# A four-layer network on one core: the split operands are placed at a different byte distance from the weights in each stage

## The chip, the core and the metric

The kernel runs as one program on one of the eight cores of a Trainium2 chip. Its time is device microseconds (us) from launch to end; lower is better. The engines named below are TensorE (PE; PEld is its weight load), VectorE (DVE), ScalarE (ACT), GpSimd (POOL) and SyncE (SP), which issues the DMAs.

## What is computed

A sequence of 256 tokens with 1024 channels goes through four residual layers, each a mixer and then a feed-forward block, all in float32:

```
for mixer, ffn in ((moba, conv_ffn), (mla, conv_ffn), (pool, conv_ffn_2), (chunk_attention, conv_ffn_2)):
    h = h + mixer(rms_norm(h))
    h = h + ffn(rms_norm(h))

def conv_ffn(xn, w_gate, conv_w, conv_b, w_up, w_down):        # 1024 -> 2816 -> 1024
    g = xn @ w_gate
    gc = conv_b + sum(conv_w[j] * shifted(g, j) for j in range(3))
    return (gelu(gc) * (xn @ w_up)) @ w_down
```

The three attention mixers have 16 heads of 64; the second works through low-rank latents (384 and 256 wide); the pool mixer takes means over 2, 4, 8 and 16 tokens and then one 256x256 product per group of channels. A final norm lies between the second and the third layer.

## The kernel before

**Stages.** The program has eight stages, numbered `A, F0, B, F1, POOL, F2, DD, F3`: A, B and DD are the attention mixers, POOL the pool mixer, F0 to F3 the feed-forward blocks. They run one after the other, since each needs the residual stream of the one before. Each engine has a hand-written program (`tensor_program`, `scalar_program`, `vector_program`, `sync_program`), and semaphores tie them together; no scheduler orders anything.

**Weights.** All weights come as 180 units of up to 128x2048 floats (1 MB). SP loads them into three buffers `raw`. ScalarE copies a unit to `whi` in the format fp32r (line 1173), VectorE writes the rest, `raw - whi`, to `wlo` (line 1712). `whi` and `wlo` are rings of five buffers of 8192 bytes per partition each.

**Split operands.** The other operand is split in the same way, each 256 columns of high part followed by 256 columns of low part: `xx` holds the stage's normalised input (8 blocks of 128 channels, lines 1176 and 1717), `hx` the activations of a feed-forward block (22 blocks, lines 1248 and 1863), `ox` the outputs of the attention heads, and in stage B the latents (8 blocks, lines 1311 and 1956). A product is high times high, plus high times low, plus low times high.

**The three ways in which TensorE takes them.** In `block_wide` (lines 463 and 465) the weights are stationary: one matmul streams the 512 columns of high and low part against 128x128 of `whi`, and one the 256 columns of the high part against `wlo`. Such a pair is the unit of almost all work in F0 to F3 and of half the output projection of the attention mixers. In `across` and `last_pair` (helper `three`, lines 422 to 424) it is three matmuls of 256 columns. In the query, key and value products of A and DD (lines 679, 680 and 686) the roles are the other way round: 128x128 of `xx` is stationary and 512 columns of `whi` or `wlo` stream. Lines 518 and 519 sum squares for the norm: `sx`, 256 columns, streams against the constant `ones_r`.

**Where the buffers lie.** Buffers follow each other in a partition in the order of the code, each at a multiple of 32 bytes. Every `whi` and `wlo` begins at a multiple of 128 bytes. `gx`, ahead of `xx`, is 8 floats longer than a multiple, so `xx` begins 32 bytes past a multiple of 128. An unused buffer of 8 floats (`pad_moving`) stands ahead of `vec`, and with it `sx`, `ones_r`, `hx` and `ox` begin 32 bytes past a multiple of 128 too. All slices that a matmul takes begin a multiple of 512 bytes further on in their buffer. "Distance" below is the start of the split operand less that of the weights, modulo 128 bytes: 32 in every stage of this kernel. `sx` and `ones_r` have the distance 0 to each other.

Of the kernel before, what the change touches and what calls it, by code (L numbers as in the profile page):

```python
# [7 lines left out]
F32 = mybir.dt.float32  # L8
F32R = mybir.dt.float32r
# [6 lines left out]
NF = 22  # L16
# [24 lines left out]
A, F0, B, F1, POOL, F2, DD, F3 = range(8)  # L41

# [58 lines left out]
def build(nc, dram, out):  # L101
    plan, first = unit_plan()
    N_UNITS = len(plan)
    with ExitStack() as ctx:
# [55 lines left out]
        xx = sb("xx", [128, KD, 2, S], F32R)  # L160
# [15 lines left out]
        hx = sb("hx", [128, NF, 2, S], F32R, ffn_mem)  # L176
# [10 lines left out]
        ox = sb("ox", [128, KD, 2, S], F32R, att_mem)  # L187
# [30 lines left out]
        TB = ctx.enter_context(nc.psum_tensor("TB", [128, 2, 512], F32))  # L218

# [43 lines left out]

        def xh(k):
            return xx[:, k, 0, :]

        def xl(k):
            return xx[:, k, 1, :]
# [151 lines left out]
        def tensor_program(e):  # L420
# [51 lines left out]
            def last_pair(s):  # L472


                b = ffn_banks(s, 5)
                for m in range(2):
                    kk = 0
                    for n, nk in zip(range(first[s] + 31, first[s] + 34), (8, 8, 6)):
                        wh, wl = unit(n)
                        if m == 0:  # L480
                            weights_here(n)
                        for k in range(nk):
                            start, stop = kk == 0, kk == NF - 1
                            if m == 0:
                                last = block_wide(n, b[:, 0, :], 0, k, hx, kk, start, stop)
                            else:
                                last = three(b[:, 1, 0:256], wh[:, k, 128:256], wl[:, k, 128:256], hx[:, kk, 0, :],
                                             hx[:, kk, 1, :], start, stop)
# [39 lines left out]
            def ffn(s):  # L528
                u = first[s]
                bg, bu = ffn_banks(s, 0), ffn_banks(s, 1)  # L530
                weights_here(u + 1)
                if s != F2:
                    e.wait_ge(s_res, n_res(s - 1, 1))
                if s == F2:
                    for k in (0, 1):
                        x_here(s, k)
                        across_wide(u, bg, k, xx, k, k == 0, False)
                    e.wait_ge(s_uu, 2)
                    for k in (0, 1):
                        across_wide(u + 1, bu, k, xx, k, k == 0, False)  # L540
                for k in range(2 if s == F2 else 0, KD):
                    x_here(s, k)
                    last = across_wide(u, bg, k, xx, k, k == 0, k == KD - 1)
                    if k == KD - 1:
                        last.then_inc(s_used, 1)
                    last = across_wide(u + 1, bu, k, xx, k, k == 0, k == KD - 1)
                    if k == KD - 1:
                        last.then_inc(s_used, 1)
                if s != F2:
                    spread_sums(s)  # L550
                for i in range(1, 11):
                    n = u + 2 * i
                    bg, bu = ffn_banks(s, 2 * i), ffn_banks(s, 2 * i + 1)
                    weights_here(n)
                    if i >= 2:
                        e.wait_ge(s_gr, n_ff(s, i - 2))
                    for k in range(KD):
                        last = across_wide(n, bg, k, xx, k, k == 0, k == KD - 1)
                        if s == F2 and i == 1 and k == 0:
                            spread_sums(s)  # L560
                    last.then_inc(s_used, 1)
                    weights_here(n + 1)
                    if i >= 2:
                        e.wait_ge(s_ub, n_ff(s, i - 2))
                    else:
                        e.wait_ge(s_sr, LAYER[s] + 1)
                    for k in range(KD):
                        last = across_wide(n + 1, bu, k, xx, k, k == 0, k == KD - 1)
                    last.then_inc(s_used, 1)
                n = u + 22  # L570
                for c in range(4):
                    b = ffn_banks(s, 2 + c)
                    e.wait_ge((s_gr, s_ub)[c % 2], n_ff(s, 9 + c // 2))
                    if c == 3:
                        last_pair(s)
                        break
                    k0 = 0
                    for j, nk in enumerate((8, 8, 6)):
                        weights_here(n)
                        for k in range(nk):  # L580
                            if c == 0:
                                e.wait_ge(s_hl, n_ff(s, (k0 + k) // 2))
                            last = across_wide(n, b, k, hx, k0 + k, k0 + k == 0, k0 + k == NF - 1)
                        last.then_inc(s_used, 1)
                        n += 1
                        k0 += nk
# [65 lines left out]
            def project(s, u, c, ks):  # L652
# [4 lines left out]
                for k in ks:  # L657
                    last = across_wide(u + c, out_banks(c), k, ox, k, k == 0, k == KD - 1)
# [3 lines left out]
            def heads_mixer(s):  # L662
# [10 lines left out]
                def high(i, h, k):  # L673
# [5 lines left out]
                    e.matmul(po, xx[:, k, 0, sl], wh[:, k % 4, :], start=k == 0, stop=False, skip_group_check=True)  # L679
                    e.matmul(po, xx[:, k, 1, sl], wh[:, k % 4, :], start=False, stop=False, skip_group_check=True)  # L680

                def low(i, h, k):
# [3 lines left out]
                    return e.matmul(slot_bank(s, i, h)[:, :], xx[:, k, 0, sl], wl[:, k % 4, :], start=False,  # L686
# [194 lines left out]
            def latent_mixer():  # L881
# [3 lines left out]
                def latent_half(i, h):  # L885
# [10 lines left out]
                    for k in range(4):  # L896
# [3 lines left out]
                        last = three(b[:, 0:w], xx[:, kk, 0, sl], xx[:, kk, 1, sl], wh[:, k, :], wl[:, k, :],  # L900
# [28 lines left out]
                def channels(n, b, col, nk, kk, at):  # L929
# [3 lines left out]
                    for m in range(2):  # L933
                        sl = slice(col + m * 128, col + (m + 1) * 128)
                        for k in range(nk):
                            last = three(po[:, m, :], wh[:, k, sl], wl[:, k, sl], ox[:, kk + k, 0, :],
                                         ox[:, kk + k, 1, :], m == 0 and k == 0, k == nk - 1)
# [12 lines left out]
                def value_block(h, c):  # L950
# [10 lines left out]
                    for k in range(2):  # L961
                        last = three(bk(s, 2 + (h if c == 0 else 0))[:, :], ox[:, 6 + k, 0, sl], ox[:, 6 + k, 1, sl], wh[:, k, :],
# [3 lines left out]
                def query_rope(h):  # L966
# [7 lines left out]
                    for k in range(3):  # L974
                        last = three(bk(s, h)[:, :], ox[:, 3 + k, 0, sl], ox[:, 3 + k, 1, sl], wh[:, k, :], wl[:, k, :],
# [44 lines left out]
                def rows(c, *ks):  # L1020

                    for k in ks:
# [4 lines left out]
                        last = across(u + 10 + c, out_bank(s, c), k, ox, k, k == 0, k == KD - 1)  # L1027
# [64 lines left out]
            def pool_mixer():  # L1092
# [22 lines left out]
                def linear(g):  # L1115
# [3 lines left out]
                    for k in (2 * g, 2 * g + 1):  # L1119
                        x_here(s, k)  # L1120
                        for h in range(2):
                            sl = slice(h * 128, (h + 1) * 128)
                            last = three(b[:, h * 256:(h + 1) * 256], xx[:, k, 0, sl], xx[:, k, 1, sl], wh[:, k, :],
# [34 lines left out]
        def scalar_program(e):  # L1158
# [16 lines left out]
            def split_x(s, k):  # L1175
                e.activation(xx[:, k, 0, :], xT[:, k, :], ACT.Copy, scale=gain_of(s, k)).then_inc(s_xh, 1)
# [63 lines left out]
            def ffn(s, func):  # L1240
# [5 lines left out]
                def finish(i):  # L1246
                    e.wait_ge(s_hb, n_ff(s, i))
                    e.activation(hx[:, 2 * i:2 * i + 2, 0, :], hb[:, :, :], ACT.Copy).then_inc(s_hh, 1)
# [60 lines left out]
            def output_hi(s, j):  # L1309
                e.wait_ge(s_av, n_pair(s, j))  # L1310
                e.activation(ox[:, j, 0, :], av_bank(s, j)[:, 0:256], ACT.Copy).then_inc(s_oh, 1)
# [162 lines left out]
            def latent_mixer():  # L1474
# [38 lines left out]
                def latent_hi(t, c):  # L1513
                    gain = vcol("b_q_norm", c) if c < 3 else vcol("b_kv_norm", c - 3)
                    e.wait_ge(s_lt, t + 1)
                    e.activation(ox[:, 3 + c, 0, :], LT[t % 3], ACT.Copy, scale=gain).then_inc(s_ch, 1)
# [179 lines left out]
        def vector_program(e):  # L1696
# [18 lines left out]
            def split_x(s, k):  # L1715
                e.wait_ge(s_xh, n_x(s, k))
                e.scalar_tensor_tensor(out=xx[:, k, 1, :], in0=xT[:, k, :], scalar=gain_of(s, k),  # L1717
                                       in1=xx[:, k, 0, :].bitcast(F32), op0=ALU.mult,
# [124 lines left out]
            def ffn(s):  # L1843
# [17 lines left out]
                def low(i):  # L1861
                    e.wait_ge(s_hh, n_ff(s, i))
                    e.tensor_tensor(hx[:, 2 * i:2 * i + 2, 1, :], hb[:, :, :],
                                    hx[:, 2 * i:2 * i + 2, 0, :].bitcast(F32), ALU.subtract).then_inc(s_hl, 1)
# [270 lines left out]
            def latent_mixer():  # L2135
# [14 lines left out]
                def latent_lo(t, c):  # L2150
                    gain = vcol("b_q_norm", c) if c < 3 else vcol("b_kv_norm", c - 3)
                    e.wait_ge(s_ch, t + 1 if t < 2 else t)
                    e.scalar_tensor_tensor(out=ox[:, 3 + c, 1, :], in0=LT[t % 3], scalar=gain,
                                           in1=ox[:, 3 + c, 0, :].bitcast(F32), op0=ALU.mult,
# [318 lines left out]
```

## Time and profile before

| | |
|---|---|
| median of 3 runs | 1072.65 us (1072.24 to 1073.18) |
| profiled execution, first to last instruction | 1070.4 us, 2.25 us under the median of the runs |
| PE busy | 1064.7 us (99%), 6536 matmuls |
| PE weight loads busy | 932.3 us (87%) |
| DVE busy | 839.0 us (78%) |
| ACT busy | 655.2 us (61%) |
| DMA | 191.67 MB, mean 179 GB/s |
| share of PE in the chain that ended last | 94% |

The profiled execution has no run time of its own on record beside its span, so the span is set against the median of the three runs; what lies between is launch and end. Matmuls are pipelined: the duration that the profile shows for one (0.39 us) overlaps the next, so the pace is read from the distance of two starts, not from durations.

### The profile page before, as it was taken

Reading aid. Unit: us, or ns where it says so; the run is one execution under the profiler, and the core shown is the slowest. Engines: PE = TensorE matmul, PEld = TensorE weight load, DVE = VectorE, ACT = ScalarE, POOL = GpSimd, SP = SyncE. Lnnn points to the kernel's source line nnn. Section 1 sums busy time; section 2 is a strip of 40 time slices with the busy share of each in tenths; the row PEclk is TensorE's granted clock in tenths of the full one; section 3 lists DMA queues with packets and bytes.
Section 4 is the critical chain, followed back from the end, with each engine's and each line's share of the span. In section 5 each row is a group of like instructions: output and inputs, shape, how many; then the busy total and the mean of one; then the engine's idle time right before and its main releaser. Section 6 shows DMA issues by size and latency. Waiting matters only on the chain.

```text
span 1070.4 us, 16292 instructions
## 1 busy us (share of the span) xinstructions
PE 1064.7 (99%) x6536; PEld 932.3 (87%) x6536; DVE 839.0 (78%) x1364; ACT 655.2 (61%) x922; POOL 1.3 (0%) x8
## 2 busy tenths in 40 slices
PE   9999999999999999999999999999999999999998
PEld 7778888888898888888889888888877788888888
DVE  7985799886668779987667999876668768997852
ACT  7666567665458766765556577654456765776540
POOL 0000000000000000000000000000000000000000
PEclk9999999999999999999999999999999999999999
DMA  9552446555426155655552466455555533665540
GB/s 339 181 180 114 156 164 233 195 186 216 163 83 252 55 180 190 230 202 181 214 195 81 151 215 229 182 217 187 187 177 182 174 106 140 236 220 190 206 142 30
DMA packets 32091, 191.67 MB, mean 179 GB/s; under 512 B 4496, under 2 KB 6160, under 8 KB 12176
## 3 DMA queue, kind: packets, MB, share of 16 engines
q1 hardware_dynamic: 32016, 190.62, 50.3%
q8 instruction: 52, 0.85, 0.3%
q14 instruction: 23, 0.19, 0.1%
HBM read 189.56 MB, written 1.05 MB: 178 GB/s over the span
## 4 chain that ended last, share of the span: by engine, by line
PE 94%; DVE 2%; ACT 2%; issue 1%; DMA 0%; SPq 0%; DVEq 0%; ACTq 0%
PE banks L463 21%; PE TB L463 12%; PE SB L463 11%; PE banks L465 11%; PE TB L465 6%; PE SB L465 6%; PE banks L679 4%; PE banks L686 4%; PE banks L680 4%; PE banks L422 3%; PE banks L424 3%; PE banks L423 3%; PE banks L636 2%; PE TB L610 2%; PE SB L597 1%
## 5 line engine op out<-in xcount | busy, mean ns | idle before, releaser
L1712 DVE TENSOR_TENSOR wlo<-raw,whi 128x2048 fp32r<-128x2048 f32 (+2 forms) x180 | 395.8, 2201 | 78.6 <-ACT whi L1173 78.5
L1173 ACT ACTIVATE whi<-raw 128x2048 fp32r<-128x2048 f32 (+2 forms) x180 | 330.5, 1840 | 81.3 <-PE TB L465 25.6
L463 PE MATMUL banks<-xx,whi 128*128 128x512 f32 x752 | 262.2, 390 | 0.2 <-DVE wlo L1712 0.2
L465 PE MATMUL banks<-xx,wlo 128*128 128x256 f32 x752 | 212.1, 282 | 0.0
L463 PEld LDWEIGHTS banks<-xx,whi 128*128 128x128 f32 x752 | 141.2, 188 | 30.0 <-DVE wlo L1712 0.5
L465 PEld LDWEIGHTS banks<-xx,wlo 128*128 128x128 f32 x752 | 142.1, 189 | 0.0
L463 PE MATMUL TB<-xx,whi 128*128 128x512 f32 x336 | 117.8, 390 | 0.2 <-DVE xx L1717 0.2
L463 PE MATMUL SB<-xx,whi 128*128 128x512 f32 x320 | 111.8, 390 | 0.0
L465 PE MATMUL TB<-xx,wlo 128*128 128x256 f32 x336 | 94.7, 282 | 0.0
L463 PE MATMUL banks<-hx,whi 128*128 128x512 f32 x264 | 91.7, 390 | 0.0
L465 PE MATMUL SB<-xx,wlo 128*128 128x256 f32 x320 | 90.2, 282 | 0.0
L1258 ACT ACTIVATE ct<-gp,vec 128x256 f32<-128x256 f32 x88 | 48.2, 595 | 63.1 <-DVE gp L1879 63.1
L679 PE MATMUL banks<-whi,xx 128*128 128x512 f32 x192 | 78.0, 406 | 0.5 <-ACT whi L1665 0.5
L680 PE MATMUL banks<-whi,xx 128*128 128x512 f32 x192 | 75.9, 395 | 0.0
L463 PEld LDWEIGHTS TB<-xx,whi 128*128 128x128 f32 x336 | 63.1, 188 | 13.5 <-issue 0.3
L465 PE MATMUL banks<-hx,wlo 128*128 128x256 f32 x264 | 74.4, 282 | 0.0
L463 PEld LDWEIGHTS SB<-xx,whi 128*128 128x128 f32 x320 | 60.1, 188 | 12.6
L465 PEld LDWEIGHTS TB<-xx,wlo 128*128 128x128 f32 x336 | 63.5, 189 | 0.0
L463 PE MATMUL TB<-hx,whi 128*128 128x512 f32 x176 | 61.2, 390 | 0.0
L463 PE MATMUL SB<-hx,whi 128*128 128x512 f32 x176 | 61.2, 390 | 0.0
L465 PEld LDWEIGHTS SB<-xx,wlo 128*128 128x128 f32 x320 | 60.5, 189 | 0.0
L463 PEld LDWEIGHTS banks<-hx,whi 128*128 128x128 f32 x264 | 49.6, 188 | 10.4
(244 smaller groups left out, 1944.6 us busy)
## 6 DMA issues: line engine op xcount, KB each, us to landing
raw<-in_gate SPq DMA_DIRECT2D x44, 1024.0 KB, 4.7
raw<-in_up SPq DMA_DIRECT2D x44, 1024.0 KB, 4.8
raw<-in_down SPq DMA_DIRECT2D x32, 1024.0 KB, 4.8
raw<-in_down SPq DMA_DIRECT2D x16, 768.0 KB, 4.2
raw<-in_d_kq SPq DMA_DIRECT2D x8, 1024.0 KB, 5.0
raw<-in_a_kq SPq DMA_DIRECT2D x6, 1024.0 KB, 5.8
raw<-in_a_o SPq DMA_DIRECT2D x4, 1024.0 KB, 4.8
raw<-in_b_o SPq DMA_DIRECT2D x4, 1024.0 KB, 5.6
```

Source lines behind the costliest of these rows:

```text
L422: e.matmul(po, ah, bh, start=start, stop=False, skip_group_check=True)
L423: e.matmul(po, ah, bl, start=False, stop=False, skip_group_check=True)
L424: return e.matmul(po, al, bh, start=False, stop=stop, skip_group_check=True)
L463: e.matmul(po[:, 0:512], wh[:, k, sl], a[:, kk, :, :].rearrange("p w s -> p (w s)"), start=start, stop=stop, skip_group_check=True)
L465: return e.matmul(po[:, 0:256], wl[:, k, sl], a[:, kk, 0, :], start=False, stop=stop, skip_group_check=True)
L610: last = e.transpose(TB[:, a, c * 128:(c + 1) * 128], sc[:, a, c * 128:(c + 1) * 128], ident)
L679: e.matmul(po, xx[:, k, 0, sl], wh[:, k % 4, :], start=k == 0, stop=False, skip_group_check=True)
L680: e.matmul(po, xx[:, k, 1, sl], wh[:, k % 4, :], start=False, stop=False, skip_group_check=True)
L686: return e.matmul(slot_bank(s, i, h)[:, :], xx[:, k, 0, sl], wl[:, k % 4, :], start=False, stop=k == KD - 1, skip_group_check=True)
L1173: e.activation(whi[n % RING][:, 0:nk * w], raw[n % RAW][:, 0:nk * w], ACT.Copy).then_inc(s_hi, 1)
L1258: e.activation(ct[:, m, :], g[:, m, 0:S], ACT.Identity, scale=cw(0, 2 * i + m), bias=cb(2 * i + m)).then_inc(s_tap, 1)
L1712: e.tensor_tensor(wlo[n % RING][:, 0:nk * w], raw[n % RAW][:, 0:nk * w], whi[n % RING][:, 0:nk * w].bitcast(F32), ALU.subtract).then_inc(s ...
```

## The change

`xx`, `hx` and `ox` become flat buffers that are 32 floats (128 bytes) longer. Each stage takes a view into them (`XX[s]`, `HX[s]`, `OX[s]`) that begins at an offset of its own, in floats, from three tables. Every read and write of the three buffers on TensorE, ScalarE and VectorE goes through the view of its stage. The number, order, shapes and waits of all instructions stay as they are. Buffers allocated behind `xx` move by 128 bytes, those behind `hx` or `ox` by 256, so their place modulo 128 bytes stays.

```diff
+SHIFT = 32
+X_AT = {A: 16, F0: 4, B: 4, F1: 8, POOL: 0, F2: 12, DD: 8, F3: 16}
+H_AT = {F0: 20, F1: 24, F2: 28, F3: 0}
+O_AT = {A: 2, B: 1, DD: 6}
...
-        xx = sb("xx", [128, KD, 2, S], F32R)
+        xx = sb("xx", [128, KD * 2 * S + SHIFT], F32R)
...
-        hx = sb("hx", [128, NF, 2, S], F32R, ffn_mem)
+        hx = sb("hx", [128, NF * 2 * S + SHIFT], F32R, ffn_mem)
...
-        ox = sb("ox", [128, KD, 2, S], F32R, att_mem)
+        ox = sb("ox", [128, KD * 2 * S + SHIFT], F32R, att_mem)
...
+        def placed(buf, n, at):
+            return buf[:, at:at + n * 2 * S].rearrange("p (k w s) -> p k w s", k=n, w=2)
+
+        XX = {st: placed(xx, KD, X_AT[st]) for st in range(8)}
+        HX = {st: placed(hx, NF, H_AT[st]) for st in (F0, F1, F2, F3)}
+        OX = {st: placed(ox, KD, O_AT[st]) for st in (A, B, DD)}
...
-                                last = block_wide(n, b[:, 0, :], 0, k, hx, kk, start, stop)
+                                last = block_wide(n, b[:, 0, :], 0, k, HX[s], kk, start, stop)
...
-                    last = across_wide(u, bg, k, xx, k, k == 0, k == KD - 1)
+                    last = across_wide(u, bg, k, XX[s], k, k == 0, k == KD - 1)
...
-                        last = across(u + c, bk(s, c), k, ox, k, k == 0, k == KD - 1)
+                        last = across(u + c, bk(s, c), k, OX[s], k, k == 0, k == KD - 1)
...
-                    e.matmul(po, xx[:, k, 0, sl], wh[:, k % 4, :], start=k == 0, stop=False, skip_group_check=True)
+                    e.matmul(po, XX[s][:, k, 0, sl], wh[:, k % 4, :], start=k == 0, stop=False, skip_group_check=True)
...
-                e.activation(xx[:, k, 0, :], xT[:, k, :], ACT.Copy, scale=gain_of(s, k)).then_inc(s_xh, 1)
+                e.activation(XX[s][:, k, 0, :], xT[:, k, :], ACT.Copy, scale=gain_of(s, k)).then_inc(s_xh, 1)
...
-                e.tensor_tensor(ox[:, j, 1, :], av_bank(s, j)[:, 0:256], ox[:, j, 0, :].bitcast(F32),
+                e.tensor_tensor(OX[s][:, j, 1, :], av_bank(s, j)[:, 0:256], OX[s][:, j, 0, :].bitcast(F32),
```

The rest of the diff puts the views in place of the buffers in the same way, and removes two unused helpers. With the 32 bytes that the buffers had already, the distances from the weights are, in bytes:

| stage | A | F0 | B | F1 | POOL | F2 | DD | F3 |
|---|---|---|---|---|---|---|---|---|
| `xx` | 96 | 48 | 48 | 64 | 32 | 80 | 64 | 96 |
| `hx` | | 112 | | 0 | | 16 | | 32 |
| `ox` | 40 | | 36 | | | | 56 | |

## Rows read from the trace of the kernel before

**Rows 1.** Page, parts 1 and 2: busy share of engines, TensorE clock
```profile
PE 1064.7 (99%) x6536; PEld 932.3 (87%) x6536; DVE 839.0 (78%) x1364; ACT 655.2 (61%) x922; POOL 1.3 (0%) x8
...
PEclk9999999999999999999999999999999999999999
```

**Rows 2.** Waits of TensorE (PE) over the whole span
```profile
PE SB L670 <- DVE ones L2297: 1.1, 1, 1.1
PE banks L679 <- ACT whi L1665: 0.5, 1, 0.5
PE banks L636 <- ACT pt L1307: 0.4, 1, 0.4
PE banks L463 <- DVE wlo L1712: 0.2, 1, 0.2
PE TB L463 <- DVE xx L1717: 0.2, 1, 0.2
```

**Rows 3.** Timeline, stage F0, PE: start us, duration us, instruction
```profile
200.13 0.39 PE L463 MATMUL TB<-xx,whi 128*128 128x512 f32 x1
200.36 0.28 PE L465 MATMUL TB<-xx,wlo 128*128 128x256 f32 x1
200.48 0.39 PE L463 MATMUL TB<-xx,whi 128*128 128x512 f32 x1
...
202.56 0.39 PE L463 MATMUL TB<-xx,whi 128*128 128x512 f32 x1
```

**Rows 4.** Timeline, end of F3, PE (line 422 begins each group of three)
```profile
1061.33 0.28 PE L422 MATMUL banks<-hx,whi 128*128 128x256 f32 x1
...
1062.38 0.28 PE L422 MATMUL banks<-hx,whi 128*128 128x256 f32 x1
```

**Rows 5.** Timeline, stage DD, PE
```profile
784.59 0.40 PE L679 MATMUL banks<-whi,xx 128*128 128x512 f32 x1
...
785.06 0.40 PE L679 MATMUL banks<-whi,xx 128*128 128x512 f32 x1
```

**Rows 6.** Groups by shape, PE: count | busy us, mean ns | idle before
```profile
L463 PE MATMUL banks<-xx,whi 128*128 128x512 f32 x752 | 262.2, 390 | 0.2 <-DVE wlo L1712 0.2
L465 PE MATMUL banks<-xx,wlo 128*128 128x256 f32 x752 | 212.1, 282 | 0.0
...
L680 PE MATMUL banks<-whi,xx 128*128 128x512 f32 x192 | 75.9, 395 | 0.0
...
L422 PE MATMUL banks<-ox,whi 128*128 128x256 f32 x136 | 39.7, 292 | 0.0
...
L422 PE MATMUL banks<-hx,whi 128*128 128x256 f32 x88 | 24.5, 279 | 0.0
...
L463 PE MATMUL SB<-ox,whi 128*128 128x512 f32 x48 | 16.9, 391 | 0.0
...
L518 PE MATMUL SB<-sx,ones_r 128*128 128x256 f32 x4 | 1.1, 281 | 0.0
```

**Rows 7.** Timeline around lines 518 and 519, stage F1, PE
```profile
400.65 0.28 PE L465 MATMUL banks<-xx,wlo 128*128 128x256 f32 x1
400.77 0.28 PE L518 MATMUL SB<-sx,ones_r 128*128 128x256 f32 x1
400.89 0.28 PE L519 MATMUL SB<-sx,ones_r 128*128 128x256 f32 x1
```

**Rows 8.** Busy time in a stretch, line 463 alone, stage F1
```profile
389.60:573.00 183.40, 175.59 (x507) 94.96 (x506) 1.00 0.54 194
```

**Rows 9.** Groups by shape, PE, stage DD alone
```profile
L680 PE MATMUL banks<-whi,xx 128*128 128x512 f32 x96 | 38.0, 395 | 0.0
```

**Rows 10.** Groups by shape, VectorE (DVE)
```profile
L1887 DVE SCALAR_TENSOR_TENSOR ct<-gp,vec,ct 128x256 f32<-128x256 f32 x88 | 38.4, 477 | 0.0
L1891 DVE SCALAR_TENSOR_TENSOR ct<-gp,vec,ct 128x256 f32<-128x256 f32 x88 | 38.4, 477 | 0.0
...
L1717 DVE SCALAR_TENSOR_TENSOR xx<-gx,vec,xx 128x256 fp32r<-128x256 f32 x48 | 21.3, 481 | 7.8 <-ACT xx L1176 7.8
```

More of the change, by code:

```diff
@@ L262, in unit @@
                     wlo[r][:, 0:nk * w].rearrange("p (k n) -> p k n", k=nk))
[L264 to L268, printed above, removed]
         def gain_of(s, k):
@@ L484, in last_pair @@
                             if m == 0:
-                                last = block_wide(n, b[:, 0, :], 0, k, hx, kk, start, stop)
+                                last = block_wide(n, b[:, 0, :], 0, k, HX[s], kk, start, stop)
                             else:
-                                last = three(b[:, 1, 0:256], wh[:, k, 128:256], wl[:, k, 128:256], hx[:, kk, 0, :],
-                                             hx[:, kk, 1, :], start, stop)
+                                last = three(b[:, 1, 0:256], wh[:, k, 128:256], wl[:, k, 128:256], HX[s][:, kk, 0, :],
+                                             HX[s][:, kk, 1, :], start, stop)
                             kk += 1
@@ L557, in ffn @@
                     for k in range(KD):
-                        last = across_wide(n, bg, k, xx, k, k == 0, k == KD - 1)
+                        last = across_wide(n, bg, k, XX[s], k, k == 0, k == KD - 1)
                         if s == F2 and i == 1 and k == 0:
@@ L567, in ffn @@
                     for k in range(KD):
-                        last = across_wide(n + 1, bu, k, xx, k, k == 0, k == KD - 1)
+                        last = across_wide(n + 1, bu, k, XX[s], k, k == 0, k == KD - 1)
                     last.then_inc(s_used, 1)
@@ L582, in ffn @@
                                 e.wait_ge(s_hl, n_ff(s, (k0 + k) // 2))
-                            last = across_wide(n, b, k, hx, k0 + k, k0 + k == 0, k0 + k == NF - 1)
+                            last = across_wide(n, b, k, HX[s], k0 + k, k0 + k == 0, k0 + k == NF - 1)
                         last.then_inc(s_used, 1)
@@ L657, in project @@
                 for k in ks:
-                    last = across_wide(u + c, out_banks(c), k, ox, k, k == 0, k == KD - 1)
+                    last = across_wide(u + c, out_banks(c), k, OX[s], k, k == 0, k == KD - 1)
                 if ks[-1] == KD - 1:
@@ L678, in high @@
                     po = slot_bank(s, i, h)[:, :]
-                    e.matmul(po, xx[:, k, 0, sl], wh[:, k % 4, :], start=k == 0, stop=False, skip_group_check=True)
-                    e.matmul(po, xx[:, k, 1, sl], wh[:, k % 4, :], start=False, stop=False, skip_group_check=True)
+                    e.matmul(po, XX[s][:, k, 0, sl], wh[:, k % 4, :], start=k == 0, stop=False, skip_group_check=True)
+                    e.matmul(po, XX[s][:, k, 1, sl], wh[:, k % 4, :], start=False, stop=False, skip_group_check=True)
                 def low(i, h, k):
@@ L685, in low @@
                     sl = slice(h * 128, (h + 1) * 128)
-                    return e.matmul(slot_bank(s, i, h)[:, :], xx[:, k, 0, sl], wl[:, k % 4, :], start=False,
+                    return e.matmul(slot_bank(s, i, h)[:, :], XX[s][:, k, 0, sl], wl[:, k % 4, :], start=False,
                                     stop=k == KD - 1, skip_group_check=True)
@@ L899, in latent_half @@
                             x_here(s, kk)
-                        last = three(b[:, 0:w], xx[:, kk, 0, sl], xx[:, kk, 1, sl], wh[:, k, :], wl[:, k, :],
+                        last = three(b[:, 0:w], XX[s][:, kk, 0, sl], XX[s][:, kk, 1, sl], wh[:, k, :], wl[:, k, :],
                                      kk == 0, kk == KD - 1)
@@ L935, in channels @@
                         for k in range(nk):
-                            last = three(po[:, m, :], wh[:, k, sl], wl[:, k, sl], ox[:, kk + k, 0, :],
-                                         ox[:, kk + k, 1, :], m == 0 and k == 0, k == nk - 1)
+                            last = three(po[:, m, :], wh[:, k, sl], wl[:, k, sl], OX[s][:, kk + k, 0, :],
+                                         OX[s][:, kk + k, 1, :], m == 0 and k == 0, k == nk - 1)
                     return last
@@ L961, in value_block @@
                     for k in range(2):
-                        last = three(bk(s, 2 + (h if c == 0 else 0))[:, :], ox[:, 6 + k, 0, sl], ox[:, 6 + k, 1, sl], wh[:, k, :],
+                        last = three(bk(s, 2 + (h if c == 0 else 0))[:, :], OX[s][:, 6 + k, 0, sl], OX[s][:, 6 + k, 1, sl], wh[:, k, :],
                                      wl[:, k, :], k == 0, k == 1)
@@ L974, in query_rope @@
                     for k in range(3):
-                        last = three(bk(s, h)[:, :], ox[:, 3 + k, 0, sl], ox[:, 3 + k, 1, sl], wh[:, k, :], wl[:, k, :],
+                        last = three(bk(s, h)[:, :], OX[s][:, 3 + k, 0, sl], OX[s][:, 3 + k, 1, sl], wh[:, k, :], wl[:, k, :],
                                      k == 0, k == 2)
@@ L1026, in rows @@
                         e.wait_ge(s_ol, n_pair(s, k))
-                        last = across(u + 10 + c, out_bank(s, c), k, ox, k, k == 0, k == KD - 1)
+                        last = across(u + 10 + c, out_bank(s, c), k, OX[s], k, k == 0, k == KD - 1)
                         if k == KD - 1:
@@ L1122, in linear @@
                             sl = slice(h * 128, (h + 1) * 128)
-                            last = three(b[:, h * 256:(h + 1) * 256], xx[:, k, 0, sl], xx[:, k, 1, sl], wh[:, k, :],
+                            last = three(b[:, h * 256:(h + 1) * 256], XX[s][:, k, 0, sl], XX[s][:, k, 1, sl], wh[:, k, :],
                                          wl[:, k, :], k == 2 * g and h == 0, k == 2 * g + 1)
@@ L1716, in split_x @@
                 e.wait_ge(s_xh, n_x(s, k))
-                e.scalar_tensor_tensor(out=xx[:, k, 1, :], in0=xT[:, k, :], scalar=gain_of(s, k),
-                                       in1=xx[:, k, 0, :].bitcast(F32), op0=ALU.mult,
+                e.scalar_tensor_tensor(out=XX[s][:, k, 1, :], in0=xT[:, k, :], scalar=gain_of(s, k),
+                                       in1=XX[s][:, k, 0, :].bitcast(F32), op0=ALU.mult,
                                        op1=ALU.subtract).then_inc(s_xl, 1)
@@ L2152, in latent_lo @@
                     e.wait_ge(s_ch, t + 1 if t < 2 else t)
-                    e.scalar_tensor_tensor(out=ox[:, 3 + c, 1, :], in0=LT[t % 3], scalar=gain,
-                                           in1=ox[:, 3 + c, 0, :].bitcast(F32), op0=ALU.mult,
+                    e.scalar_tensor_tensor(out=OX[s][:, 3 + c, 1, :], in0=LT[t % 3], scalar=gain,
+                                           in1=OX[s][:, 3 + c, 0, :].bitcast(F32), op0=ALU.mult,
                                            op1=ALU.subtract).then_inc(s_cl, 1)
```

16 lines of the change are left out of this document (8 added, 8 removed).

## The prediction

> **What bounds the kernel now.** I read the page first: TensorE is busy for 99% of the span, and its granted clock is full, 1.0, which is the 2.4 GHz level, in all 40 slices [rows 1]. Then the waits of TensorE. They name all that it ever waited for, and the five of them sum to 1.1 + 0.5 + 0.4 + 0.2 + 0.2 = 2.4 us [rows 2]. So no producer, buffer or DMA decides anything here; the time is the pace at which TensorE takes its matmuls, and a change can show only if it changes that pace or makes a new wait longer than the slack that now hides it.
>
> The pace is in the timeline. In F0 seven pairs (512 columns against `whi`, then 256 against `wlo`) begin between 200.13 and 202.56, which is 0.347 us a pair; the first takes 0.23 and the second 0.12 [rows 3]. At one column per cycle of 2.4 GHz, 768 columns would take 0.320 us, so a pair loses 0.027 us, 8%. The groups of three at the end of F3 take 0.35 us for 768 columns (three groups in 1.05 us) [rows 4], and the mixer products with the roles reversed 0.47 us for two matmuls of 512 columns, 0.235 us each [rows 5]. All pay 8 to 10% over the column count. What this change can touch is this surplus: it alters neither the number nor the order of instructions, only where the streamed operand starts against the stationary one.
>
> **The change, part by part.** *TensorE.* The question is whether the distance between the two operands sets the surplus. The trace before has three cases. Distance 32 with the weights stationary: 390 ns for 512 columns, 282 ns for 256 in a pair, 279 ns for 256 in a group of three. The same buffers with the roles reversed, so that the weights stream: 395 ns for 512 columns. And distance 0, `sx` against `ones_r`: 281 ns for 256 columns [rows 6]. In the timeline that matmul starts 0.12 us after its predecessor and its successor 0.12 us after it, as for every other matmul of 256 columns [rows 7]. So going from distance 32 to 0 shows nothing above 2 or 3 ns on 256 columns, and there are only four such matmuls, each in the midst of others. I take 0 ns per matmul for every new distance, since the only other distance in the trace is the one nearest to a test of the change.
>
> The bounds. Above: the largest step that the rows show between two placements or roles is 5 ns on 512 columns (395 less 390) and 3 ns on 256 (282 less 279) [rows 6]. All pairs but those on `hx` in F3 and all the reversed products get a new distance. The four feed-forward blocks have some 506 pairs each (the stretch of F1 holds 507 of line 463, one at its edge) [rows 8], the mixers 2 x 48 on `ox` [rows 6], so 2120 in all, and 154 of them (`hx` in F3, 7 passes of 22) stay: 1966 pairs x 8 ns = 15.7 us. The reversed products are 3 x 96 in DD [rows 9] and as many in A: 576 x 5 ns = 2.9 us. Together +18.6 us, if every distance but 32 paid the full step. Below: the whole surplus of 27 ns a pair [rows 3] taken back in every pair would be -53 us; in a single block of 506 pairs, -13.7 us. I take 0 between these ends, since the row at distance 0 lies on the present pace, and not between it and either end.
>
> The Trainium skill speaks on both sides. "SBUF — State Buffer" (section "SBUF: two separate sides") gives TensorE a second independent read port for the weight load, by which the distance would not matter at all and the sum stays 0. The same page (Specifications) says that each cross to a new 16-byte line pays a penalty. All offsets of `xx` and `hx` keep the number of such lines, but `ox` at 36, 40 and 56 bytes takes one line more per stream; an estimate from that page, one line in 64 of some 80 us of `ox` streams, is 1.3 us. No run here shows it yet.
>
> *ScalarE and VectorE.* They write the buffers and VectorE reads the high part back. VectorE reads `gp` 4 bytes on in line 1887 and 8 bytes on in line 1891: both take 477 ns, and the same shape written into `xx` 481 ns [rows 10]. So 0 ns for an odd start. If an access to `ox` were slower all the same, VectorE is busy 78% and ScalarE 61% of the span [rows 1], and TensorE's wait for them sums to 2.4 us [rows 2]; that slack is the cover. Without it, 24 pieces of `ox` in three mixers would have to be some 90 ns slower each to reach 2.2 us.
>
> *DMA and memory.* No DMA touches the three buffers. The buffers behind them move by 128 or 256 bytes, so nothing changes modulo 128.
>
> The sum is 0. The profiled execution spans 1070.4 us, 2.25 us under the median of the runs, and I forecast the median: 1072.7 us.
>
> **The rivals.** *Slower, by the distance 0.* The weight load of the next matmul runs while the present one streams, and two readers at the same place in a line or bank could hold each other up. Three uses land on a multiple of 64 bytes: `xx` and `hx` in F1 and `xx` in DD. For it speaks that the surplus exists at all and is the same in every feed-forward block, which all have one distance; against it the matmul at distance 0 [rows 6, 7]. Price with the steps above: 506 pairs x 8 ns = 4.0 us, and 288 x 5 ns = 1.4 us, so 1078.1 us. The place to see it is F1 against F0. It decides from about 4 ns a pair on, where it reaches 2.1 us, 0.2%; that is about what a measurement of this kernel can tell from no change. Chance 0.20.
>
> *Slower, as every distance but 32 pays.* Then every block but the `hx` part of F3 slows, up to 1072.7 + 18.6 = 1091.3 us; at half the step, 1082. Chance 0.12.
>
> *Slower, by the offsets of `ox` alone*, which are the only ones that are no multiple of four floats. No matmul in the trace streams from such a start. If those streams went at half pace, 96 pairs x 0.347 and 3 x 136 matmuls x 0.117 us [rows 3, 4, 6] would come a second time, +81 us; a tenth of it would be 1080.8 us. VectorE's indifference to such starts [rows 10] speaks against it. Chance 0.08.
>
> *Faster.* The distance 32 may be a poor one. If one of the new distances freed a block of its surplus, this block would go from 0.347 to 0.320 us a pair, -13.7 us, 1059 us; a tenth of the surplus in all pairs would be -5.3 us, 1067.4 us. The trace speaks against it only by the matmul at distance 0, which is no faster. The skill's "TensorE: Matmul & The Clock Gate" (section "Back-to-back issue gap") gives N/2.4 + 2.5 ns for a matmul, 325 ns for a pair by an estimate from it; the trace's 347 disagrees, so something does hold fp32r back. Chance 0.14.
>
> *No change*, within 0.2%: 0.46, the forecast.
>
> **How the numbers follow.** Faster has the 0.14 of its case, no change 0.46, and slower 0.20 + 0.12 + 0.08 = 0.40. For the range I leave out about half of the faster case (below 1067) and the worse half of the second and third case (above 1085), some 0.17 in all: 1067 to 1085 us. The forecast's own range is 1070.6 to 1074.8.
>
> **What would show it.** Right: a pair takes 0.347 us in F0, F1, F2 and F3 alike, the mixers keep 0.235 us and 0.117 us, and each stage has the length that it has now. The first rival shows as F1 longer than F0 with DD longer than A, at an unchanged mean for lines 422 to 424 on `ox`; the second as an even stretch of all blocks with the `hx` part of F3 at the old pace; the third as longer means of the rows on `ox` alone; the last as a block whose pair comes nearer to 0.320 us. The forecast is wrong if any block's pair moves by more than 4 ns, or if a wait of TensorE for `ox` or `xx` above 2 us appears that is not there now.

## The result and the profile after

The changed kernel takes 1083.01 us (median of 3 runs, 1082.39 to 1083.21) against 1072.65 us: ratio 1.0096, 95% interval 1.0082 to 1.011. It is slower by 10.4 us, 1%. The profiled execution spans 1080.6 us, 10.2 us more than before.

Parts 1 and 2 of the page after, engines and clock, answer to [rows 1]:

```profile
PE 1075.6 (100%) x6536; PEld 932.8 (86%) x6536; DVE 839.7 (78%) x1364; ACT 655.1 (61%) x922; POOL 1.3 (0%) x8
...
PEclk9999999999999999999999999999999999999999
```

The waits of TensorE after, all that there are, answer to [rows 2]:

```profile
PE SB L676 <- DVE ones L2303: 1.1, 1, 1.1
PE banks L642 <- ACT pt L1313: 0.3, 1, 0.3
PE TB L469 <- DVE xx L1723: 0.2, 1, 0.2
```

TensorE is still busy all the time, at the same clock and with the same 6536 matmuls, but for 10.9 us longer (1075.6 less 1064.7); its waits are 1.6 us in place of 2.4. The busy time of VectorE and ScalarE is the same within 0.7 us. So nothing waits for anything new: the matmuls themselves are taken more slowly. The lines have moved by 6: 463, 465, 422, 518 and 680 are now 469, 471, 428, 524 and 686. The groups by shape after (count | busy us, mean ns), which answer to [rows 6]:

```profile
L469 PE MATMUL banks<-xx,whi 128*128 128x512 f32 x752 | 265.4, 395 | 0.1
L471 PE MATMUL banks<-xx,wlo 128*128 128x256 f32 x752 | 210.8, 280 | 0.0
...
L469 PE MATMUL banks<-hx,whi 128*128 128x512 f32 x264 | 92.6, 394 | 0.0
...
L686 PE MATMUL banks<-whi,xx 128*128 128x512 f32 x192 | 76.3, 397 | 0.0
...
L428 PE MATMUL banks<-ox,whi 128*128 128x256 f32 x136 | 40.0, 294 | 0.0
...
L524 PE MATMUL SB<-sx,ones_r 128*128 128x256 f32 x4 | 1.1, 280 | 0.0
```

The 512 columns of a pair have gone from 390 to 395 ns on `xx` (394 on `hx`), the 256 columns from 282 to 280; the reversed product from 395 to 397. Durations overlap, so the pace is better read from starts. In the timeline of F1 after (start us, duration us), on `hx`, the first and the twelfth 512-column matmul of a run:

```profile
529.82 0.40 PE L469 MATMUL TB<-hx,whi 128*128 128x512 f32 x1
...
533.71 0.40 PE L469 MATMUL TB<-hx,whi 128*128 128x512 f32 x1
```

Eleven pairs in 3.89 us are 0.3536 us a pair, where [rows 3] give 0.347. The same reading over every pair of a stage, and over all other matmuls on the three buffers, says where the 10.2 us went. Change of the summed times from start to start, in us:

| | A | F0 | B | F1 | POOL | F2 | DD | F3 | sum |
|---|---|---|---|---|---|---|---|---|---|
| on `xx` | +0.46 | +1.20 | +0.04 | +2.31 | -0.16 | +1.05 | +0.07 | +1.17 | +6.1 |
| on `hx` | | +1.05 | | +1.24 | | 0.00 | | +0.05 | +2.3 |
| on `ox` | +0.53 | | +1.05 | | | | +0.26 | | +1.8 |

The sum, 10.3 us, is the whole difference. Every stage with a new distance pays, except F2 on `hx` (distance 16); the products with the roles reversed, on `xx` in A, B and DD, pay little. The groups of three pay most for their length: between the starts of two groups on `ox` there were 350.0 to 351.0 ns and are now 360.2 (A, DD) and 361.2 ns (B), and on `hx` in F1 there are 360.0 for 350.0.

### The profile page after: what moved, and what is told of

Same layout as the page of the kernel before. It is cut to its first block, busy times and chain, and to the rows that moved or that the text cites. A ratio compares the mean times of both kernels' runs of the same rounds, so it can differ in the third digit from the quotient of the medians.

```text
span 1080.6 us, 16292 instructions
## 1 busy us (share of the span) xinstructions
PE 1075.6 (100%) x6536; PEld 932.8 (86%) x6536; DVE 839.7 (78%) x1364; ACT 655.1 (61%) x922; POOL 1.3 (0%) x8
## 3 DMA queue, kind: packets, MB, share of 16 engines
HBM read 189.56 MB, written 1.05 MB: 176 GB/s over the span
## 4 chain that ended last, share of the span: by engine, by line
PE 97%; DVE 1%; ACT 1%; issue 0%; DVEq 0%
PE banks L469 21%; PE TB L469 12%; PE SB L469 12%; PE banks L471 11%; PE TB L471 6%; PE SB L471 6%; PE banks L685 4%; PE banks L686 4%; PE banks L692 4%; PE banks L428 3%; PE banks L429 3%; PE banks L430 3%; PE banks L642 2%; PE TB L616 2%; PE SB L603 1%; PE banks L761 1%
## 5 line engine op out<-in xcount | busy, mean ns | idle before, releaser
L469 PE MATMUL banks<-xx,whi 128*128 128x512 f32 x752 | 265.4, 395 | 0.1
L469 PE MATMUL TB<-xx,whi 128*128 128x512 f32 x336 | 119.1, 395 | 0.2 <-DVE xx L1723 0.2
```

The costliest lines, as they stand in the source:

```text
L469: e.matmul(po[:, 0:512], wh[:, k, sl], a[:, kk, :, :].rearrange("p w s -> p (w s)"), start=start, stop=stop, skip_group_check=True)
```

## The experiments

The theory: TensorE's pace depends on where the streamed operand begins relative to the weights. The rivals: it depends on the absolute place of the streamed operand; the longer buffers and higher addresses do it; one reader alone (the load of the next weights, or the matmul's own weights) sets the loss. "A pair" below is the mean time from one 512-column start to the next, over all pairs of the stage named that follow each other directly, from the starts in that run's trace; three or four pairs of F2 that hold a wait or the sums of the norm are left out. All medians stand beside runs of the kernel before on the same chip, 1072.4 to 1072.5 us.

**Longer buffers alone.**

```diff
-X_AT = {A: 16, F0: 4, B: 4, F1: 8, POOL: 0, F2: 12, DD: 8, F3: 16}
-H_AT = {F0: 20, F1: 24, F2: 28, F3: 0}
-O_AT = {A: 2, B: 1, DD: 6}
+X_AT = {A: 0, F0: 0, B: 0, F1: 0, POOL: 0, F2: 0, DD: 0, F3: 0}
+H_AT = {F0: 0, F1: 0, F2: 0, F3: 0}
+O_AT = {A: 0, B: 0, DD: 0}
```

> The changed kernel with all three tables at 0: the buffers are longer and what lies behind them has moved by 128 and 256 bytes, but every distance is 32 as before. If the distance modulo 128 bytes sets the pace, or the absolute place modulo 128 does: 1072.7 us, a pair (512 and 256 columns) at 0.347 us. If the lengthening itself, by higher address bits, made the loss: near 1083 us.

Measured: 1072.91 us, ratio 1.0004 (0.9995 to 1.0014). The lengthening costs nothing; the offsets do it. `xx` keeps 228.4 + 118.3 ns a pair to the tenth. `hx`, which the longer `xx` has moved by 128 bytes, splits its pair differently, 229.2 + 117.5, with the same sum: a first sign that a step of 128 bytes is not nothing.

**Distance 0 modulo 128 bytes everywhere.** The same tables with 24 floats in every entry.

> All tables at 24 floats, so every split operand lies at a multiple of 128 bytes, as the weights do: distance 0 in every stage. The changed kernel's F1 had 353.4 ns a pair at the distances 64 and 0 against 346.7 before. If that is the distance and not the stage: 2120 pairs x 6.7 ns and some 670 single matmuls of 256 columns x 3 ns, +16 us, 1089 us, with F0, F2 and F3 as slow as F1. If the stage made it, only F1 is slow: near 1077 us.

Measured: 1084.37 us, ratio 1.011 (1.0095 to 1.0125). The loss is there and in all four feed-forward blocks alike (+2.65 to +2.79 us each), so it is the distance and not the stage; it is 11.8 us and not 16. The groups by shape show why:

```profile
L469 PE MATMUL banks<-xx,whi 128*128 128x512 f32 x752 | 265.4, 394 | 0.1
L471 PE MATMUL banks<-xx,wlo 128*128 128x256 f32 x752 | 212.7, 283 | 0.0
...
L469 PE MATMUL banks<-hx,whi 128*128 128x512 f32 x264 | 93.5, 399 | 0.0
...
L428 PE MATMUL banks<-hx,whi 128*128 128x256 f32 x88 | 24.9, 283 | 0.0
...
L524 PE MATMUL SB<-sx,ones_r 128*128 128x256 f32 x4 | 1.1, 282 | 0.0
```

`xx` and `hx` are both at a multiple of 128 bytes from the weights, but `xx` at 128 modulo 256 and `hx` at 0, and they differ: 394 against 399 ns, a pair 351.1 against 353.4 ns. So 128 bytes is not the period, or the buffer counts too; the next run decides for the first. The groups of three on `hx` take 360.0 ns in place of 350.0.

**The weights moved, the split operands left at 32 bytes past a multiple of 128.**

```diff
+        off_line("weights")
         whi = [sb(f"whi{i}", [128, UNIT], F32R) for i in range(RING)]
...
+        sb("pad_back", [128, 24])
         xx = sb("xx", [128, KD, 2, S], F32R)
```

> The kernel of before, with the weight rings moved by 32 bytes and the split operands left at 32 bytes past a multiple of 128 (two unused buffers are added): distance 0, absolute place of the streamed operand unchanged. If the distance between the two operands decides: as slow as the run with distance 0 everywhere, about 1089 us. If the absolute place of the streamed operand decides: 1072.7 us.

Measured: 1082.86 us, ratio 1.0095 (1.0078 to 1.0111). The groups by shape, on `xx`:

```profile
L465 PE MATMUL banks<-xx,whi 128*128 128x512 f32 x752 | 265.5, 394 | 0.1
L467 PE MATMUL banks<-xx,wlo 128*128 128x256 f32 x752 | 212.7, 283 | 0.0
```

The split operands lie 32 bytes past a multiple of 128 as before, and the loss is there: `xx` and `hx`, both at 128 modulo 256 from the weights here, take 351.1 ns a pair, what `xx` took in the run before at the same distance with the weights elsewhere. The padding has moved the split operands too, by 128 bytes; that their new place, 160 modulo 256, is not what costs is shown by the run with longer buffers alone, where `hx` lies there at 346.7 ns.

**Everything moved together.**

```diff
+        off_line("all")
         raw = [sb(f"raw{i}", [128, UNIT]) for i in range(RAW)]
```

> The kernel of before with an unused buffer of 32 bytes ahead of everything: weights at 32 and split operands at 64 bytes past a multiple of 128, distance 32 kept. If the distance decides: 1072.7 us. If the absolute place of the streamed operand decides: the place is that of F1 in the changed kernel less 0 to 32 bytes, some 3 to 7 ns a pair, 1079 to 1088 us.

Measured: 1072.49 us, ratio 0.9999 (0.999 to 1.0008). The groups by shape:

```profile
L464 PE MATMUL banks<-xx,whi 128*128 128x512 f32 x752 | 262.2, 390 | 0.2 <-DVE wlo L1713 0.2
L466 PE MATMUL banks<-xx,wlo 128*128 128x256 f32 x752 | 212.1, 282 | 0.0
```

The rows are those of [rows 6] to the nanosecond. Weights at 32 and split operands at 64 past a multiple of 128 are as good as 0 and 32. With the run before this answers the question for a shift of 32 bytes: the distance between the two operands decides, the absolute place of neither does. Other shifts were not tried.

**Two sweeps.** Buffers 64 floats longer, each stage at a distance that no run had had.

```diff
+SHIFT = 64
+X_AT = {A: 28, F0: 20, B: 32, F1: 28, POOL: 24, F2: 36, DD: 32, F3: 40}
+H_AT = {F0: 44, F1: 48, F2: 58, F3: 62}
+O_AT = {A: 60, B: 62, DD: 32}
```

> A second sweep, with the buffers 64 floats longer, at distances (modulo 256 bytes) that no run has had: xx 144 in A, 112 in F0, 160 in B, 144 in F1, 128 in POOL, 176 in F2, 160 in DD, 192 in F3; hx 208, 224, 8 and 24 in F0 to F3; ox 16, 24 and 160 in A, B and DD. If the pace is a function of the distance alone, hx at 8 and 24 stays between 346.5 and 353.4 ns a pair, since 0 gave 353.4, 16 and 32 gave 346.7; 160 stays at 346.5. If the period is 128 bytes, 144 equals 16 (346.7), 176 equals 48 (349.9), 192 equals 64 (353.3), 208 equals 80 (350.5). If it is 256, they may differ. In all some 1076 to 1084 us.

```diff
+SHIFT = 64
+X_AT = {A: 60, F0: 57, B: 60, F1: 59, POOL: 56, F2: 61, DD: 62, F3: 62}
+H_AT = {F0: 63, F1: 1, F2: 2, F3: 3}
+O_AT = {A: 61, B: 59, DD: 63}
```

> A sweep in steps of 4 bytes around the two fast distances 16 and 32: xx 16 in A and B, 4 in F0, 12 in F1, 20 in F2, 24 in DD and F3; hx 28, 36, 40 and 44 in F0 to F3; ox 20, 12 and 28 in A, B and DD. If only the distance in whole lines matters, all between 16 and 32 are as fast as these two, 346.7 ns a pair. If a start inside a line of 16 bytes costs by itself, every one but 16 and 32 is slower, as ox at 36 was in the changed kernel (353 ns). If there is a better distance than 32, it shows as a pair below 346.5 ns. In all 1070 to 1082 us.

Measured, one run each: 1083.75 and 1084.08 us, both near or above the upper end of what was expected. All pairs of the feed-forward blocks, from these two, the runs above, the changed kernel and the last run below, ordered by the distance modulo 256 bytes (`hx` lies at 32 in the kernel before, and at 240, 0, 16 and 160 in F0 to F3 of the changed one):

| distance | ns a pair | distance | ns a pair | distance | ns a pair |
|---|---|---|---|---|---|
| 0 | 353.4 | 36 | 356.6 | 128 | 351.1 |
| 4 | 359.4 | 40 | 346.9 | 144 | 346.7 |
| 8 | 353.3 | 44 | 346.7 | 160 | 346.7 |
| 12 | 346.7 | 48 | 350.1 | 176 | 350.0 |
| 16 | 346.7 | 64 | 353.3 | 192 | 353.2 |
| 20 | 355.6 | 80 | 350.0 | 208 | 350.0 |
| 24 | 353.9, 359.8 | 96 | 350.0 | 224 | 346.7 |
| 28 | 343.4 | 112 | 353.2 | 240 | 353.2 |
| 32 | 346.7 | | | 156 | 346.7 to 347.2 |

The fewer pairs on `ox` repeat most of these values: at 12, 16, 20, 24 and 28 they take 346.7, 347.0, 355.4, 353.3 and 343.5 ns.

The values don't slide, they step: all but three (20, 128, and 24 on `xx`) lie within 0.5 ns of 343.4, 346.7, 350.0, 353.3, 356.6 or 359.8, levels some 3.3 ns apart. Why there are steps no run shows.

A start at no multiple of 16 bytes is not bad by itself: 12, 28, 40 and 44 are fast, 4, 20, 24 and 36 are the slowest of all. The worst is `hx` at 24 in F3, here as groups by shape of that stretch:

```profile
L469 PE MATMUL banks<-hx,whi 128*128 128x512 f32 x51 | 18.4, 402 | 0.0
...
L471 PE MATMUL banks<-hx,wlo 128*128 128x256 f32 x50 | 14.1, 283 | 0.0
```

That is 402 ns where [rows 6] have 390. The best is `hx` at 28 in F0, in the timeline of the fine sweep:

```profile
253.36 0.39 PE L469 MATMUL TB<-hx,whi 128*128 128x512 f32 x1
...
256.79 0.39 PE L469 MATMUL TB<-hx,whi 128*128 128x512 f32 x1
```

Ten pairs in 3.43 us, 0.343 us a pair.

**One ring moved alone.**

```diff
+        off_line("lo")
         wlo = [sb(f"wlo{i}", [128, UNIT], F32R) for i in range(RING)]
...
+        sb("pad_back", [128, 56])
         xx = sb("xx", [128, KD, 2, S], F32R)
```

> The kernel of before with the wlo ring moved by 32 bytes and the split operands moved by 256 bytes: distance 32 to whi, 0 to wlo. If a matmul is slowed by the load of the next weights that runs under it: the 512 columns stream while wlo loads, so they take some 236 ns in place of 228, the 256 columns stay at 118; a pair 353 to 355, 1085 to 1090 us. If a matmul is slowed by the place of its own weights: the 512 columns stay at 228 ns and the 256 columns slow by some 4 ns, 1081 us.

Measured: 1068.37 us, ratio 0.9961 (0.9947 to 0.9975): faster than before, which neither theory had. Ten pairs of F0 in the timeline:

```profile
149.80 0.39 PE L465 MATMUL banks<-xx,whi 128*128 128x512 f32 x1
...
153.25 0.39 PE L465 MATMUL banks<-xx,whi 128*128 128x512 f32 x1
```

3.45 us, 0.345 us a pair. Over the stage the 512 columns take 226.4 ns (228.4 before) and the 256 columns 118.1 (118.3), from start to start.

```diff
+        off_line("hi")
         whi = [sb(f"whi{i}", [128, UNIT], F32R) for i in range(RING)]
...
+        sb("pad_back", [128, 56])
         wlo = [sb(f"wlo{i}", [128, UNIT], F32R) for i in range(RING)]
```

> The converse: whi moved by 32 bytes, wlo and the split operands by 256: distance 0 to whi, 32 to wlo. If the load of the next weights under a matmul slows it: the 512 columns stay at 228 ns, the 256 columns, under which the next whi loads, take 116 to 122 ns; a pair 345 to 350, 1070 to 1080 us. If the place of its own weights does: the 512 columns take some 236 ns, the 256 columns 118, 1085 to 1090 us.

Measured: 1085.4 us, ratio 1.0121 (1.0106 to 1.0136). Ten pairs of F0:

```profile
149.63 0.40 PE L465 MATMUL banks<-xx,whi 128*128 128x512 f32 x1
...
153.17 0.40 PE L465 MATMUL banks<-xx,whi 128*128 128x512 f32 x1
```

3.54 us. The 512 columns take 232.9 ns and the 256 columns 120.4: both are slower, the first less than the theory of a matmul's own weights had it (236), the second more (118). The load of the next weights alone is refuted by both runs: `wlo` at distance 0 under the 512 columns did no harm. The matmul's own weights alone are refuted by the run with `wlo` moved. What fits is that the two distances act together. In both runs the rings also lie 32 bytes apart from each other, modulo 256, and that was not tested apart from the rest.

**28 for every pair.**

```diff
+SHIFT = 64
+X_AT = {A: 62, F0: 63, B: 0, F1: 63, POOL: 56, F2: 63, DD: 62, F3: 63}
+H_AT = {F0: 63, F1: 63, F2: 63, F3: 63}
+O_AT = {A: 63, B: 63, DD: 63}
```

> All distances at the best that the sweeps showed: xx 28 in the feed-forward blocks, 24 in A and DD, 32 in B and 0 in POOL; hx and ox 28 everywhere. The one stage that had 28 before, hx in F0 of the fine sweep, took 343.8 ns a pair against 346.7. If the distance alone decides and xx behaves as hx: 2120 pairs x 2.9 ns = 6.1 us and about 1 us in A and DD less, 1065.5 us. If 28 was good only for that stage or buffer: 1070 to 1078 us.

Measured: 1064.48 us, ratio 0.9925 (0.991 to 0.994): 8 us faster than the kernel before, 18.5 us faster than the changed one. It beats both. The groups by shape, and a run of eleven pairs on `hx` in the timeline of F1:

```profile
L469 PE MATMUL banks<-xx,whi 128*128 128x512 f32 x752 | 259.8, 388 | 0.3 <-DVE wlo L1718 0.3
L471 PE MATMUL banks<-xx,wlo 128*128 128x256 f32 x752 | 208.3, 277 | 0.0
...
L428 PE MATMUL banks<-ox,whi 128*128 128x256 f32 x136 | 39.3, 289 | 0.0
```

```profile
529.71 0.39 PE L469 MATMUL SB<-hx,whi 128*128 128x512 f32 x1
...
533.49 0.39 PE L469 MATMUL SB<-hx,whi 128*128 128x512 f32 x1
```

388 and 277 ns for 390 and 282, and 3.78 us for eleven pairs, 0.3436 us each; over whole stages it is 343.3 to 343.5 ns on all three buffers. The groups of three gain nothing: the first matmul of a group on `ox` shows 289 for 292 ns, but from the start of one group to the next there are 351.1 to 351.3 ns on `ox` and 351.1 on `hx`, for 350.0 to 351.0 and 350.0 before. So the best distance for pairs is not the best for every form. A and DD, with `xx` at 24, have the reversed products at 231.0 and 230.8 ns from start to start, for 233.1.

**`wlo` moved, and a sweep.** The wiring of the run at 1068.4 us with tables of its own.

> The wlo ring 32 bytes further on than whi, as in the run at 1068.4 us, and a sweep of the distance to whi: xx 28 in A and F0, 32 in B, 44 in F1, 0 in POOL, 60 in F2, 56 in DD, 16 in F3; hx 36, 48, 64 and 12 in F0 to F3; ox 28, 60 and 44. The distance to wlo is 32 less each time. If a pair's time were the sum of one part set by the distance to whi and one by the distance to wlo, then 28 would keep the good pace of about 344 and 44 and 12 that of 346; if it is the two together, as the two runs with one ring moved suggest, any of them can lie between 343 and 360. In all 1068 to 1085 us.

Measured, one run: 1073.62 us. Distances to `whi` / `wlo` and ns a pair: 28/252 344.4, 44/12 346.7, 60/28 346.6, 16/240 344.6, 36/4 360.0, 48/16 348.9, 64/32 348.8, 12/236 346.8. None beats 28/28 (343.4). Most lie near the pace that the distance to `whi` has in the table, whatever the one to `wlo`: 0 to 2 ns from it at 12, 16, 28, 44 and 48, 3 to 5 ns at 36 and 64. So the distance to `whi` seems to weigh more, which fits the two runs before (32/0 344.5, 0/32 353.3), but the other is not without weight.

**`xx` back at 32.**

```diff
-X_AT = {A: 16, F0: 4, B: 4, F1: 8, POOL: 0, F2: 12, DD: 8, F3: 16}
+X_AT = {st: 0 for st in range(8)}
```

> The changed kernel with the table of xx at 0, so that only hx and ox keep their new distances. In the two traces the matmuls on xx took 6.1 us of the 10.3, those on hx 2.3 and those on ox 1.8. If the parts simply add: 1072.7 + 4.2 = 1076.9 us. If one part's loss depends on the other's place: elsewhere.

Measured: 1075.29 us, ratio 1.0026 (1.0016 to 1.0036). The parts don't add: 2.8 us are left, and 4.2 were to be. Most of the difference is in one place. `hx` in F1 lies at the same distance 0 as in the changed kernel, and the timeline has:

```profile
530.18 0.39 PE L469 MATMUL SB<-hx,whi 128*128 128x512 f32 x1
...
533.64 0.39 PE L469 MATMUL SB<-hx,whi 128*128 128x512 f32 x1
```

Ten pairs in 3.46 us, 0.346 a pair (346.7 ns over the stage), where the changed kernel had 353.3 on the same addresses. All that differs in the kernel is the place of `xx`, whose stream runs before it: at 32 and not at 64. `hx` in F1 costs 0.2 us here and 1.2 us there; in F2 it even gains 0.2 us. There the same addresses give the same 346.7 ns in both kernels but split otherwise, 227.6 + 119.1 in the changed kernel and 225.1 + 121.6 here. So at one distance the stream has at least two steady rhythms; that the stream ahead of it decides which one it holds is argued from one trace of each kernel. The two values at 24 in the table (353.9 and 359.8) may be the same thing, though there the buffers differ too; that was not tried.

**The same, 128 bytes on.**

```diff
+SHIFT = 64
+X_AT = {A: 30, F0: 31, B: 32, F1: 31, POOL: 24, F2: 31, DD: 30, F3: 31}
+H_AT = {F0: 31, F1: 31, F2: 31, F3: 31}
+O_AT = {A: 31, B: 31, DD: 31}
```

> The run at 1064.5 us with every distance but 128 bytes other: 156 for 28, 152 for 24, 160 for 32, 128 for 0. If only the distance modulo 128 bytes counts: 1064.5 us, a pair at 343.5 ns. If the place modulo 256 counts too, as the small difference between the distances 0 (353.4 ns) and 128 (351.1 ns) hints: a pair 1 to 3 ns off, 1066 to 1071 us.

Measured: 1073.4 us, ratio 1.0008 (0.9998 to 1.0017), worse than either case expected. The groups by shape:

```profile
L469 PE MATMUL banks<-xx,whi 128*128 128x512 f32 x752 | 262.7, 393 | 0.2 <-DVE wlo L1718 0.2
L471 PE MATMUL banks<-xx,wlo 128*128 128x256 f32 x752 | 209.1, 278 | 0.0
```

The 512 columns take 392 or 393 ns, not 388, and a pair 346.7 to 347.2 ns for 343.4. All that 28 had gained is gone at 156. The pairs on `ox`, at 156 too, take 353.4 ns in A and B but 347.6 in DD, on the same addresses within one trace. In DD they begin with three pairs at 353 or 354 ns and then go over to some 347: two rhythms at one distance, and a passage from one to the other. The period is more than 128 bytes. The kernel before had `xx` at 32 and `hx` at 288 modulo 512 with the same 346.7 ns, and the run with the weights moved had `xx` at 128 and `hx` at 384 with the same 351.1; both fit 256, but no run was made to test it.

## Why the prediction was right or wrong

The time, 1083.0, lies in the range (1067 to 1085), near its upper end, but not where the forecast put it: 1072.7, no change, with a chance of 0.46. Slower had 0.40. That the range held is owed to the room that it left for the rivals, and not to the reasoning behind the forecast, which had the mechanism wrong.

**What bounds the kernel: right.** TensorE's pace and nothing else. Waits, clock, counts and the other engines stayed; the whole 10.3 us is in the starts of its matmuls. *ScalarE and VectorE*, taken at 0 with their slack as cover, and *DMA and memory*, taken at 0, were right; the run with longer buffers alone shows the second.

**The step that failed: "I take 0 ns per matmul for every new distance, since the only other distance in the trace is the one nearest to a test of the change."** It rested on `sx` against `ones_r`, four matmuls at distance 0 with the usual 281 ns [rows 6]. They have 280 ns in the changed kernel as well, and 282 in the run where everything lies at distance 0 modulo 128 and each pair loses 4 to 7 ns. From start to start they take 118 ns before and in that run, where a matmul of a group of three on `hx` goes from 116.7 to 120.0 ns. So two matmuls in a row, with other weights loading around them, did not show what a stream pays at that distance: the loss is in the steady rhythm of matmul and weight load, and that rhythm was in the trace at one distance only. Measured in place of 0: +3.3 to +6.7 ns a pair at 48, 64, 80, 96, 240 and 0, 10 to 11 ns a group of three on `ox` at 164, 168 and 184 (36, 40 and 56 modulo 128), and 0 a pair at 16 and 160. The stretch of `hx` in F3, counted as unchanged, had moved from 32 to 160 modulo 256; it happened to cost nothing.

**The bounds held for this change.** Above, 8 ns a pair and 5 ns a reversed product, +18.6 us; the largest in the changed kernel was 6.7 ns a pair. The groups of three were left out of the bound, though they have the largest step, 10 to 11 ns. Other distances pass the bound for pairs, 13 ns at 24. Below, the surplus of 27 ns a pair: 28 took back 3.3 of it.

**The rivals.** The second, that every distance but 32 pays, at half the step 1082 us, came out almost to the number; it had 0.12. Its mechanism is not exact: 12, 16, 44, 144, 160 and 224 pay nothing and 28 gains. The first had the right stage at the top, F1, at 3.6 us for the 4.0 predicted; its 5.4 us would have been half of the loss, and DD, where it put 1.4 us, lost 0.07 on `xx`. Its bar of 2.1 us at 4 ns a pair is 2.0 (506 pairs), which changes nothing. The third had `ox`: +1.8 us, where half pace would be +81 and a tenth of that 8. The estimate of 1.3 us from the Trainium skill's "SBUF — State Buffer" (Specifications, the line of 16 bytes) is near that in size (it takes one line in 64 for all of `ox`, where a stream of 512 columns is 128 such lines), but the runs don't bear out its reason: 12, 28 and 44, which take one line more, are as fast as 16 and 32 or faster.

**The Trainium skill's rule of independent read ports** (the same page, "SBUF: two separate sides") would have made the distance irrelevant. The runs with the weights moved and with everything moved disagree with it: 1082.9 against 1072.5 us. Whether the ports share something behind them, and what, no run here shows. That the distance between the two operands sets the pace is shown; that it does so by the streamed reads and the weight loads meeting is argued from those two runs. The mechanism stays open: the runs with one ring moved refute both simple forms, and whether the writes of VectorE and ScalarE take part was not tried.

**What was said to show it** did in part: F1 stood out over F0, and pairs moved by more than 4 ns in F0 on `hx` and in F1. But DD did not grow over A and the rows on `ox` did not keep their mean, as the first rival wanted, and the blocks did not stretch evenly, as the second did. The faster case, at 0.14, was not this change's, but the reason given for it, that 32 may be a poor distance, holds in so far as 28 is 0.75% better; with both rings at one distance, nothing else that was tried beats 32.

## What to carry to other kernels

Where TensorE streams fp32r without a pause, the distance in bytes between the streamed operand and the weights is a parameter worth some per cent of its time: here a pair took from 343.4 to 360 ns. Don't reason it out; sweep it, several distances in one kernel with one per stage, then run the winner in all stages, since a stage's pace can also depend on what ran before it, and since pairs and groups of three don't have the same best distance. Keep both rings and the split buffers at a fixed distance modulo 256 bytes at least, and check it again when any buffer ahead of them changes size. A few matmuls at another distance in a trace don't price a stream at it.

## What was not expected of the hardware

- Steps of 4 bytes matter: 24, 28, 32 and 36 take 353.9 (or 359.8), 343.4, 346.7 and 356.6 ns a pair, and nearly all paces lie on levels 3.3 ns apart.
- 28 and 156 differ by 3 ns a pair though they are only 128 bytes apart; the kernels with all distances 128 bytes apart differ by 8.9 us (1064.5 against 1073.4 us).
- The same addresses of `hx` ran at 353.3 or 346.7 ns a pair in two kernels that differ in the place of `xx` alone, and those of `ox` at 353.4 or 347.6 in two stages of one kernel.
- `wlo` 32 bytes further on than `whi`, at distance 0 from the streamed operand, gained 4 us; `whi` at distance 0 with `wlo` at 32 lost 13 us.
- With the roles reversed, the 512 columns of weights streaming, the distance matters less: some 231 to 234 ns from start to start, as a mean over A or DD, at all distances tried.
